# Last attention with stationary values, squares of the input added without a wait, and last transposes dealt between the compression nets' slabs

## The reference: what is computed

```python
h = rms_norm(x, norm_mix[0]) * (1.0 + sc1) + sh1        # first step of all: needs the sum of x squared
...
kc = rms_norm_2(compress(kv_heads(kcr), cmp_pos_k, cmp_w1_k, cmp_w2_k), k_cmp_norm_g)
vc = compress(kv_heads(vcr), cmp_pos_v, cmp_w1_v, cmp_w2_v)      # gelu(blocks @ w1) @ w2, twice: the nets
...
o_cmp = softmax(q kc^T) vc ;  o_slc = softmax(qr k_slc^T) v_slc ;  o_win = softmax(qr k_win^T) v_win
attn = (g0 * o_cmp + g1 * o_slc + g2 * o_win) * silu(z_a)        # 8 heads of 64, g = sigmoid gates
y = gelu(s5_mixer(u, ...)) ;  ssm = y * sigmoid(y @ glu_w + glu_b) * silu(z_s)
return x + gate * (concatenate([attn, ssm]) @ w_out)
```

## Time and profile before

| what | value |
|---|---|
| three runs | 1831.61, 1834.03 (median), 1835.37 us |
| profiled execution | 1832.71 us, of which the profile's span is 1830.5 us |
| PE busy | 1757.2 us (96%), 9361 matmuls |
| DVE, ACT, POOL busy | 1166.0, 666.9, 101.2 us |
| chain that ended last | PE 80%, DVE 12%, ACT 4%, issue 2%, DMA 2% |
| TensorE clock granted | 0.992 of full speed, mean of the span |

### The profile page before, as it was taken

The page is one execution under the profiler, slowest core; times in us unless marked ns, Lnnn a source line. Parts: engine busy times, 40 slices in busy tenths (PEclk is TensorE's granted clock), DMA queues, the critical chain, the costliest instruction groups (busy, mean ns, idle before and its releaser), DMA issues.

```text
span 1830.5 us, 24238 instructions
## 1 busy us (share of the span) xinstructions
PE 1757.2 (96%) x9361; PEld 1462.1 (80%) x9361; DVE 1166.0 (64%) x2381; ACT 666.9 (36%) x1081; POOL 101.2 (6%) x194
## 2 busy tenths in 40 slices
PE   3998999999999999999999999999999998989999
PEld 3776769888888888888888898888888987777787
DVE  6877766876467656565454458874677579445574
ACT  3423673423232333233131335232423332365432
POOL 0001100001000100100000000010001100000000
PEclk9999999999999999999999999999999999999999
DMA  9354314336333534652423224454336222300351
GB/s 367 119 184 161 116 52 162 139 115 187 121 115 138 171 113 160 215 181 73 159 72 139 91 81 157 141 179 162 127 127 210 95 86 95 135 24 24 141 195 46
DMA packets 45470, 245.98 MB, mean 134 GB/s; under 512 B 6256, under 2 KB 6480, under 8 KB 27440
## 3 DMA queue, kind: packets, MB, share of 16 engines
q1 hardware_dynamic: 24848, 155.36, 23.6%
q0 software_dynamic: 20512, 89.11, 14.5%
HBM read 229.23 MB, written 15.22 MB: 134 GB/s over the span
## 4 chain that ended last, share of the span: by engine, by line
PE 80%; DVE 12%; ACT 4%; issue 2%; DMA 2%; SPq 0%; DVEq 0%; ACTq 0%
PE ps L474 69%; DVE w_lo L1481 3%; PE ps L936 2%; PE ps L810 1%; DMA ada_raw<-in_ada 1%; PE ps L917 1%; ACT w_hi L1051 1%; DVE ada_raw L1505 1%; PE ps L926 1%; DVE ada_first L1866 1%; PE ps L645 1%; DVE pre L1598 1%; PE ps L654 1%; PE ps L668 1%; PE ps L958 1%
## 5 line engine op out<-in xcount | busy, mean ns | idle before, releaser
L1481 DVE TENSOR_TENSOR w_lo<-w_raw,w_hi 128x2048 fp32r<-128x2048 f32 x136 | 311.6, 2291 | 139.2 <-ACT w_hi L1051 138.8
L474 PE MATMUL ps<-h_hi,w_hi 128*128 128x512 f32 (+1 forms) x1008 | 378.4, 375 | 11.8 <-DVE w_lo L1481 8.4
L1051 ACT ACTIVATE w_hi<-w_raw 128x2048 fp32r<-128x2048 f32 x136 | 260.1, 1913 | 355.6 <-PE ps L474 332.9
L474 PE MATMUL ps<-h_lo,w_hi 128*128 128x512 f32 (+1 forms) x1008 | 373.7, 371 | 0.0
L474 PE MATMUL ps<-h_hi,w_lo 128*128 128x512 f32 (+1 forms) x1008 | 373.3, 370 | 0.0
L474 PEld LDWEIGHTS ps<-h_hi,w_hi 128*128 128x128 f32 x1008 | 191.0, 190 | 45.8 <-DVE w_lo L1481 9.5
L474 PEld LDWEIGHTS ps<-h_hi,w_lo 128*128 128x128 f32 x1008 | 191.0, 189 | 32.7
L474 PEld LDWEIGHTS ps<-h_lo,w_hi 128*128 128x128 f32 x1008 | 191.3, 190 | 30.9
L474 PE MATMUL ps<-hid_hi,w_hi 128*128 128x512 f32 (+1 forms) x576 | 211.3, 367 | 0.0
L474 PE MATMUL ps<-hid_hi,w_lo 128*128 128x512 f32 (+1 forms) x576 | 210.6, 366 | 0.0
L474 PE MATMUL ps<-hid_lo,w_hi 128*128 128x512 f32 (+1 forms) x576 | 210.6, 366 | 0.0
(11 more groups left out here) (395 smaller groups left out, 2403.7 us busy)
## 6 DMA issues: line engine op xcount, KB each, us to landing
w_raw<-in_slabs SPq DMA_DIRECT2D x136, 1024.0 KB, 4.8
ada_raw<-in_ada POOLq DMA_DIRECT2D x104, 512.0 KB, 5.2
s_tables<-s_tab POOLq DMA_DIRECT2D x4, 2692.0 KB, 9.2
s_t<-s_tables POOLq DMA_DIRECT2D x4, 2692.0 KB, 9.7
ada_first<-in_ada SPq DMA_DIRECT2D x16, 512.0 KB, 15.0
a_bias<-in_a_bias POOLq DMA_DIRECT2D x16, 256.0 KB, 3.1
xT<-in_xT SPq DMA_DIRECT2D x4, 512.0 KB, 6.1
s_toeplitz<-KTp POOLq DMA_DIRECT2D x32, 64.0 KB, 3.3
```

The lines of the kernel that those rows point to most:

```text
L474: last = mm(o, l, r, start=start and n == 0, stop=stop and n == 2)
L1051: A(w_hi[s][:], w_raw[:, s, :], ACT.Copy).then_inc(sem("hi_done"), 1)
L1481: tt(w_lo[s][:], w_raw[:, s, :], w_hi[s][:].bitcast(F32), ALU.subtract).then_inc(sem("lo_done"), 1)
```

## The change

**Start.** DVE's waits for `consts_in` and `ones_set` move from ahead of the additions to behind them, and ACT's wait for `ones_set` moves behind the squares and `silu(0)`.

**Nets.** The turning of `h_qn` and `h_kr` (24 transposes) moves behind net 0's first slab, that of `h_qr` (16) behind net 1's first slab. DVE's ten copies are dealt between the splits, and `blocks(1)` comes behind `hT`'s copy.

**Last attention.** It takes the form of the first attention: DVE normalizes the probabilities ahead of the transposes (`h_p` gets eight buffers, and the gate is part of the factor), values run for two units at once with 64 columns of `hv` stationary for each group and 128 columns of `h_pt` moving, and all branches add up in one bank of a head pair. The compressed attention's probabilities are scaled likewise and its values (`compressed_out`) end in the same bank. So `h_o`, `c_t`, `h_q4` and the 16 transposes of `h_o` are gone, and gating with `za` and splitting into `o_hi` and `o_lo` happen in steps of the attention. Transposes come six steps behind the scores and not three, values eight and not four. The side slabs run in two bursts of 12 matmuls in neighbouring steps, and `U_STEPS` and `CMP_STEPS` are spread.

**Behind it.** `attention_part(0)` runs between `states(0)` and `outputs(0)`, and the others are dealt 1, 2, 2, 1, 1. `silu(zs)` no longer stands behind `o_hi`'s four pieces there.

```diff
-        SIDE_A, SIDE_H = Side([0, 8, 14, 20, 26, 30, 34, 38], TT, 2), Side([1, 11, 22, 33, 44, 55], 2)
+        SIDE_A, SIDE_H = Side([0, 8, 14, 20, 26, 30, 34, 38], TT, 2), Side([1, 11, 22, 33, 44, 55], 2, 2)
         A_KEPT = [41 + i for i in range(A_EARLY)]
         KCT_STEP = 4
-        U_STEPS = {step: (n // 3, n % 3) for n, step in enumerate((15, 16, 17, 19, 20, 21, 24, 25, 26, 28, 29, 30))}
-        CMP_STEPS = {step: (n // 3, n % 3) for n, step in enumerate((6, 9, 13, 23, 27, 31, 35, 38, 41, 46, 50, 57))}
-        CMP_ADD = {16 * i + 22: i for i in range(4)}
-        ZA_STEP = SIDE_H.starts[1] + 2
+        U_STEPS = {step: (n // 3, n % 3) for n, step in enumerate((8, 16, 18, 20, 27, 29, 38, 40, 49, 51, 58, 60))}
+        CMP_STEPS = {step: (n // 2, n % 2) for n, step in enumerate((6, 14, 25, 31, 36, 42, 47, 53))}
+        CMP_SCALE = {step + 4: i for step, (i, part) in CMP_STEPS.items() if part == 0}
+        OUT_STEPS = {16 * i + 22: i for i in range(4)}
+        ATT_PARTS = (1,), (2, 3), (4, 5), (6,)
+        ZA_STEP = SIDE_H.starts[1] + 3
...
             slab_t(H)
             pe.wait_ge(sem("hq_done"), 1)
-            for i in range(4):
-                transposes([h_qn[:, t, i * P:(i + 1) * P] for t in range(TT)], "hx_full")
             pe.wait_ge(sem("hk_done"), 1)
-            for i in range(2):
-                transposes([h_kr[:, t, i * P:(i + 1) * P] for t in range(TT)], "hx_full")
-            for i in range(4):
-                transposes([h_qr[:, t, i * P:(i + 1) * P] for t in range(TT)], "hx_full")
 
             for kind in range(2):
...
+                    if (kind, half) == (0, 0):
+                        for i in range(4):
+                            transposes([h_qn[:, t, i * P:(i + 1) * P] for t in range(TT)], "hx_full")
+                        for i in range(2):
+                            transposes([h_kr[:, t, i * P:(i + 1) * P] for t in range(TT)], "hx_full")
+                    if (kind, half) == (1, 0):
+                        for i in range(4):
+                            transposes([h_qr[:, t, i * P:(i + 1) * P] for t in range(TT)], "hx_full")
...
+            def compressed_out(i):
+
+                pe.wait_ge(sem("side_free"), C_COPIED[i])
+                for it in range(TT):
+                    last = mm(ps[5 + i % 2][:, it * P:(it + 1) * P], vblk[:, it % 2, :], c_pt[i % 2][:, it // 2, :],
+                              start=False, stop=True, skip_group_check=True)
+                last.then_inc(sem("c_out"), 1)
...
-            for s in range(NUH + 4):
...
+            for s in range(NUH + 7):
...
-                u = s - 3
+                u = s - 6
...
-                u = s - 4
-                if 0 <= u < NUH:
-                    i, it, br, g = UNITS_H[u]
-                    pe.wait_ge(sem("hpt_ready"), u + 1)
-                    if u % 4 == 0 and u >= 8:
-                        pe.wait_ge(sem("ho_done"), u // 4 - 1)
-                    o, vc = ps[5 + u // 4 % 2][:, (u % 4) * HD:(u % 4 + 1) * HD], slice((br - 1) * P + g * HD, (br - 1) * P + (g + 1) * HD)
+                u = s - 8
+                if u >= 0 and s % 2 == 0:
+                    i, it, br, _ = UNITS_H[u]
+                    pe.wait_ge(sem("hpt_ready"), u + 2)
+                    if u % 16 == 0 and i >= 2:
+                        pe.wait_ge(sem("hxo_gated"), i - 1)
                     for j in range(it + 1):
-                        last = mm(o, h_pt[:, u % 3, j * P:(j + 1) * P], hv[:, j, vc], start=j == 0, stop=j == it)
+                        for g in range(H_GROUPS):
+                            vc = slice((br - 1) * P + g * HD, (br - 1) * P + (g + 1) * HD)
+                            last = mm(ps[5 + i % 2][HD * g:HD * g + HD, it * P:(it + 1) * P], hv[:, j, vc],
+                                      h_pt[:, (u + g) % 3, j * P:(j + 1) * P], start=it == 0 and br == 1 and j == 0, stop=False, skip_group_check=True)
...
+                    if o == 0:
+                        pe.wait_ge(sem("hx_done"), k + 1)
...
             states(0)
-            pe.wait_ge(sem("h_added"), 4)
-            for i in range(4):
-                transposes([h_o[:, t, i * P:(i + 1) * P] for t in range(TT)], "hxo_full")
+            attention_part(0)
+            c.add("bank", 4)
             for blk in range(NBLK):
                 outputs(blk)
                 if blk + 1 < NBLK:
                     states(blk + 1)
-                    if blk == 0:
-                        pe.wait_ge(sem("hx_done"), 4)
-                    attention_part(2 * blk)
-                    attention_part(2 * blk + 1)
-                else:
-                    attention_part(2 * blk)
+                for o in ATT_PARTS[blk]:
+                    attention_part(o)
...
-            act.wait_ge(sem("ones_set"), 2)
...
+            act.wait_ge(sem("ones_set"), 2)
...
-            dve.wait_ge(sem("consts_in"), 80)
-            dve.wait_ge(sem("ones_set"), 2)
             for k in range(1, KT):
                 dve.wait_ge(sem("nsq0"), k + 1)
                 wait(dve, "nacc0", k - 1)
...
+            dve.wait_ge(sem("consts_in"), 80)
+            dve.wait_ge(sem("ones_set"), 2)
...
+            for kind in range(2):
+                hidden = ps_of(c)
                 c.add("bank")
...
                 split()
                 c.add("slab")
                 if kind == 0:
-                    blocks(1)
+                    turned_x(0)
+                    turned_x(1)
                 split()
+                for i in range(2, 6) if kind == 0 else range(6, 10):
+                    turned_x(i)
                 dve.wait_ge(sem("slab_used"), c("slab", 1))
-                free(cp(hT[:, kind, :], ps_of(c)[0:2 * CMP_PAD, 0:256]))
-                c.add("bank")
+                free(cp(hT[:, kind, :], hidden[0:2 * CMP_PAD, 0:256]))
                 c.add("slab")
                 freed()
                 V.engine_nop().then_inc(sem("hT_copied"), 1)
                 if kind == 0:
+                    blocks(1)
                     split_blocks(1)
...
+                u = s - 3
+                if 0 <= u < NUH and s % 2:
+                    i, it, br, _ = UNITS_H[u]
+                    n, h2 = P * (it + 1), slice(u % 8, u % 8 + 2)
+                    dve.wait_ge(sem("he_done"), u + 2)
+                    step(V.reciprocal(row_inv[:, h2], row_sum[:, h2]))
+                    step(tt(h_w[:, h2], row_inv[:, h2], h_gts[:, it, 6 * i:6 * i + 6].rearrange("p (g b) -> p g b", b=N_BR)[:, :, br], ALU.mult))
+                    for v in (u, u + 1):
+                        ts_(h_p[:, v % 8, 0:n], h_p[:, v % 8, 0:n], h_w[:, v % 8:v % 8 + 1], None, ALU.mult).then_inc(sem("hp_ready"), 1)
+                if s - 2 in OUT_STEPS:
+                    i = OUT_STEPS[s - 2]
+                    dve.wait_ge(sem("za_done"), 1)
+                    dve.wait_ge(sem("c_out"), i + 1)
+                    if i:
+                        dve.wait_ge(sem("hx_done"), i)
+                    tt(h_gate[:], ps[5 + i % 2][:], za[:, i, :], ALU.mult).then_inc(sem("hxo_gated"), 1)
+                if s - 4 in OUT_STEPS:
+                    i = OUT_STEPS[s - 4]
+                    dve.wait_ge(sem("hxo_hi"), i + 1)
+                    tt(o_lo[:, i, :], h_gate[:], o_hi[:, i, :].bitcast(F32), ALU.subtract).then_inc(sem("hx_done"), 1)
```

More of the change, by code:

```diff
@@ L349, in program @@
         ZA_READ = len(SIDE_A.starts) + 1 + H_USES.index(SIDE_H.starts[1]) + 1
+        C_COPIED = [len(SIDE_A.starts) + 1 + H_USES.index(step) + 1 for step, (i, part) in CMP_STEPS.items() if part == 1]
         SIDE_ALL = len(SIDE_A.starts) + 1 + len(H_USES)
@@ L898, in compressed @@
                     last.then_inc(sem("c_full"), 1)
-                elif part == 1:
-                    pe.wait_ge(sem("c_exp"), i + 1)
+                else:
+                    pe.wait_ge(sem("c_scaled"), i + 1)
                     for h in range(2):
@@ L903, in compressed @@
                     last.then_inc(sem("c_turned"), 1)
-                else:
-                    for h in range(2):
-                        last = mm(ps[7][:, 256 * h:256 * h + 256], c_pt[:, h, :], vblk[:], start=True, stop=True)
-                    last.then_inc(sem("c_out"), 1)
-            for s in range(NUH + 4):
+            def compressed_out(i):
[5 more added lines that the diff above has]
+            for s in range(NUH + 7):
                 if s < NUH and s % 2 == 0:
@@ L1388, in place_z @@
                 return za[:, 2 + u, :] if u < 2 else zs[:, u - 2, :]
-            for s in range(NUH + 3):
+            for s in range(NUH + 10):
                 side(SIDE_H, s, place_z)
@@ L1415, in _ @@
                     act.wait_ge(sem("hs_done"), s + 1)
-                    if s % 4 == 0 and s >= 8:
-                        act.wait_ge(sem("hw_done"), s // 4 - 1)
-                    A(h_p[:, s % 5, 0:n], h_p[:, s % 5, 0:n], ACT.Exp, bias=neg_max[:, s % 8:s % 8 + 1], scale=-1.0,
```

(39 more changed lines are left out.)

102 lines of the change are left out of this document (33 added, 69 removed).

## The result

The changed kernel takes 1817.23 us (median of four runs, 1814.58 to 1819.87), the kernel before 1833.4 (four runs, one more than the prediction had): 0.9913 of it, 95% interval 0.9897 to 0.9929, or 16.2 us less. The profiled execution took 1814.58 us with a span of 1812.7, the shortest of the four; against the profiled one of before it is 18.1 us shorter, by its span 17.8.

The account below looks back on a forecast made before the run. PE, busy 96% of the span, was taken as the bound, with time to win where it idles, runs at the low clock or overspends. Terms -4.5 - 8.3 - 5.5 - 2.2 = -20.5 gave 1813 us, range 1803 to 1823.

Parts of the forecast that it names:

- Start: Kernel start: without the wait for `bv_g`, DVE's first product and everything behind it come 4.5 us earlier (bounds 0 to 4.8).
- Nets: Compression nets: the new order removes most stalls and the low clock, 49.8 to 41.5 us, -8.3 (bounds -5.5 to -9).
- Attention: Last attention: new form -6, fewer waits -2.5, new costs +1.4, +1.0 and +0.6; sum -5.5, within -17 and +2.
- the 3.1 us behind `silu(za)` "stay": Last attention: values' 3.1 us wait for ACT's `h_pt`, where `silu(za)` and its table loads hold ACT, is unchanged.
- Behind: Behind the last attention: `outputs(1)` starts 22.0 us after `states(0)` and not 24.2, -2.2 (bounds -1 to -3).
- values cost half: Rival, last attention: PE overlaps both column groups without loss, up to -17 there, about -31 in all, 1803 us; chance 0.13.
- Given back: Rival: split waits and low clock in nets or attention's first steps, and a load pacing the start, leave -11, 1823; chance 0.20.
- DVE bounds the attention: Rival, last attention: normalization delays the next mask every odd step, about 1.1 us per pair, +35 us, 1848 us; chance 0.03.

Follow-up runs that it names:

- e1: Kernel before with the start change alone (ACT's and DVE's first waits for the constants moved behind the squares and their additions): 1830.02 us, 0.9987.
- e9: Kernel before with `silu(za)` of the last attention left out, a copy of one column in its place: 1830.92 us, 0.9989 of before.
- e10: Changed kernel with `silu(za)` of the last attention left out, a copy of one column in its place: 1813.86 us, 0.9889 of before.
- e4: Changed kernel with `silu(za)` of the last attention at step 22, ahead of that step's slab copy, and not at step 14: 1811.98 us, 0.9881 of before.
- e5: Changed kernel with two loops of the last attention's values swapped, all key tiles of one head before the other's: 1825.27 us, 0.9954 of before.
- e7: Kernel before with `silu(za)` at step 22, ahead of that step's slab copy, and not at step 13: 1835.24 us, 1.0017 of before.
- e8: Kernel of e4 with ACT's high part of the last attention's first slab moved ahead of the key norm: 1809.15 us, 0.9869 of before.

## Why the prediction held, and which term was off

The forecast was 1813 us (1806 to 1820) in a range of 1803 to 1823; 1817.2 lies in both. None of the four terms gave more than its forecast: by the profiles they add up to 16.2 us and not 20.5, and most of what is missing is in one of them, the attention. That the profiled execution is 17.8 shorter all the same is luck with the clock ahead of the nets. By its steps:

- **Start, forecast -4.5, measured -4.0.** The wait for `bv_g` set the pace, and the panel's first matmul moved from 28.7 to 24.7 (forecast 24.1). That the gain holds to the end is likely and not shown (e1). The size was off by the squares: I let two squares follow the fourth piece of x, to 11.9. Squares and additions wait for each other, and four of these turns behind the third piece end at 12.28.
- **Nets, forecast -8.3, measured -7.7 in the profiled execution and usually -6.5.** The wait before the uT slab was 0.78 where the forecast had 0.8. But that rests on a load of 4.8 us, the median of all 136, and in eight of nine profiles this one load took 6.0 to 6.4; then PE waits 1 us longer and 1.6 go to the lower clock. The trace of before had 6.3 for this very load. That is the lower bound that the text gave (5.5 with one fall of the clock), and it is nearer to the usual case than the value taken.
- **Attention, forecast -5.5, measured -2.4.** This is the term that was mis-sized. Its main step, that the new form is worth what the first attention shows and not half of the values, stood in size: with ACT's block out of both kernels the attention is 5.5 shorter. What failed is the step that the 3.1 us behind `silu(za)` "stay". In the changed kernel the block comes at step 14, behind both bursts of the slab, with nothing long left for PE: it waits 1.9 and 2.2 and the clock falls. The block's price went from 2.6 to 5.7 (e9, e10), and moving it beside a burst took all of this back (e4).
- **Behind, forecast -2.2, measured -2.1:** 22.07 us, where 22.0 was worked out. The terms given for it (8.4, 5.4, 3.8, 4.6) add up to 22.2.

One reading of the prediction is wrong: the 65.59 us that it gives for DVE in the first attention are the next column's, those of the weight loads (PEld). DVE has 72.63 of 102.1 us. The argument that the multiplications stay hidden is a little weaker by it and still held: in the changed kernel DVE is busy 80.72 of 136.95 us, where about 85 were expected.

The rivals: *values cost half* did not come; PE does overlap the two halves (e5), but that brings 6 us in all and none where a head has one or two key tiles. *Given back* named the mechanism that did occur, a stall in the attention's first steps and the clock behind it, at another place (ACT's block, not a split) and for 3.1 us, not for 9; 1817.2 is 4 us from the forecast's centre and 6 from this rival's. *DVE bounds the attention*: PE waits 3.4 us for the mask; a second set of multiplications, 17.4 us of DVE, costs 6.4 us of attention and not its full length, so the first had not reached that point.

The Trainium skill, TensorEngine Tiling (Array Packing), section Overview, has a speedup of up to two for a dimension of at most 64. The trace agrees with this only as an upper end: for the longest pair the new form takes 1.02 us against 1.70, of which running beside each other gives 1.51 to 1.02, and this brings nothing for one or two tiles.

What stays open is why this one load took 4.89 us once and 6 in the twelve other profiles, and what sets the clock in the attention's first 25 us, which was 0.86, 0.93 or 1.00 in kernels that differ little there.

## What to carry to other kernels

When a pipeline is deepened or its side work is dealt anew, look at every long block of the helper engines (here 4.9 us of ACT with two table loads) and ask what PE has in hand at the new place: the same block cost 2.6, 5.7 and next to nothing in three places. Put such a block just ahead of PE's longest burst that needs nothing of that engine, and check that no small copy for that burst stands behind it (e7). A load that lands "just in time" by the median of all such loads can be late in nearly every execution: read the row of the one load that the new order will wait for (here 6.3 us and not 4.8), and cost the term with the fall of the clock. And before a few microseconds are read from two single traces at a late marker, see how far that marker moves between executions of which nothing ahead of it was changed (here 2.8 us).

## What was not expected of the hardware

A longer stall can cost more behind it than it is longer: ahead of the uT slab 0.78 us of waiting left the 24 matmuls at full speed, 1.77 us made them take 7.33 and not 5.68. The busy share of PE alone doesn't tell the clock: three windows of the attention's beginning in which PE is busy 8.7 to 8.9 of 10 us had granted clocks of 0.66 (e4), 0.83 (the changed kernel) and 1.00 (e8).

The gain of matmuls that write alternate halves of the partitions depends on how many records stand in a row (two for each product): none for 8 or fewer, 0.26 us for 12 (1.14 and 0.88), 0.49 for 16.
